# Two transformer blocks on one core: norm updates in two halves of the tokens, and a second output unit issued ahead

## Chip, cores and metric

The kernel runs on one core of one Trainium2 chip. The metric is device time in microseconds (us); the median of three runs before the change is 2707.68 us (2707.38 to 2710.1).

## The reference, cut to what matters

512 tokens of width 1024 go through two layers of a first block and then through a second block. Everything is fp32. In the first block the result of each matrix is normed before it is added to the residual, and the sum is normed again for the next matrix; these two norms with the addition between them are the "sandwich":

```python
def rms_norm(x, g):
    y = x * lax.rsqrt(jnp.mean(x * x, axis=-1, keepdims=True) + EPS)
    return y * g

for l in range(2):                                   # first block
    h = rms_norm(x, attn_pre_g[l])
    proj = h @ w_in[l]                               # q, k, v of 8 head pairs, and the forget logits
    ...                                              # 4 differential and 4 forgetting head pairs -> mixed
    x = x + rms_norm(mixed @ w_out[l], attn_post_g[l])
    h = rms_norm(x, ffn_pre_g[l])
    y = (silu(h @ w_gate[l]) * (h @ w_up[l])) @ w_down[l]
    x = x + rms_norm(y, ffn_post_g[l])
# second block: x += mixer(rmsnorm(x)); x += (relu(rmsnorm(x) @ w1) ** 2) @ w2, twice
# (first mixer: stick-breaking attention, "SB"; second: gated recurrence, "HG")
```

## The kernel before, in words

**Layout.** Activations lie transposed: the width of 1024 is 8 tiles (KD) of 128 partitions, with the 512 tokens (S) along the free dimension, so each tile is 128x512. A "unit" is one 128-column slice of a weight matrix. It needs 8 k-tiles, and each k-tile takes three fp32r matmuls of 128x512 (high part of the weight with high part of the input, high with low, low with high), 24 in all, into one PSUM bank (`products`, L625).

**Weights.** SP loads a unit's raw weights into one of two slots (`load`, L451), and may do so once the slot's low part before was made. GpSimd rounds them to `w_hi` (`round_unit`, L570, instruction L576), when the unit that used `w_hi` in that slot is done. VectorE makes `w_lo = w_raw - w_hi` (`split_low`, L1167) at a place in its hand-written order, and TensorE waits for that. At a stage's start two more units are kept in `ex_hi`/`ex_lo` (`round_extra`, `split_extra`, L1162) so that four units can be computed side by side.

**Queues.** Each engine runs a program in a fixed order; semaphores join them. So an instruction that waits holds everything behind it on its engine.

**The sandwich.** In the output stage and in the last part of the FFN's down stage VectorE takes each unit out of PSUM into `yT` (`take_y`, L1361), ScalarE squares it, VectorE adds the square to `square_sum` (L1139). After the eighth, TensorE sums over partitions with a matrix of ones (`sum_squares`, L694; an fp32 matmul, issued as two instructions), ScalarE makes `rstd` with Ln and Exp (L1740), and VectorE runs `update_x` (L1344): for each tile j scale `yT` (L1351), low part of the tile before (L1148), every second time the pair of squares (L1156), and add to `xT` (L1359). ScalarE makes `h_hi` and the square of each new tile (L1747). TensorE consumes the tiles in `side_by_side` (L675): units 0 and 1 in the banks acc0 and acc1 at once, units 2 and 3 (the extra ones) in `po` and `sc` or `tp`, three and four tiles behind (LAGS), and between them the four pair sums of the next norm (L646).

**Behind the sandwich.** After the attention's sandwich comes the gate stage: `gate_up` on VectorE (L1382) takes gate and up of one FFN tile, through a chain with four activations on ScalarE; TensorE's unit pair n+1 needs the weights that VectorE splits inside the `gate_up` of the pair before (L1387, L1397). After the FFN's sandwich comes the next layer's attention (or SB): TensorE issues the forget logits' products and the rotation of q and k (L832), VectorE takes q and k (`take_qk`, L1260).

**Stage ends.** `early_output` (L668) makes the first two output units of a mixer, a and b, before the last head pair's output is there: the first 21 matmuls of a and 9 of b are spread over the last pair's work, and the rest follows as `a[21:] + b[9:]`. a[21:] waits for the last head pair (`low_output` L1278, `sb_low` L1489, `hg_low` L1701).

Of the kernel before, what the change touches and what calls it, by code (L numbers as in the profile page):

```python
# [68 lines left out]
def aux_uses():  # L69

    uses = []
    for p in range(-1, PAIRS):
        for k in range(SLOTS):
            if p == -1 and k == 3:
                uses.append("norm_att")
# [8 lines left out]
    uses += ["norm_att_post", "norm_ffn", "norm_ffn_post"]  # L84
# [18 lines left out]
A_M1 = A_SB + 3 * PAIRS + 1  # L103
# [4 lines left out]
LAGS = [0, 0, 3, 4]  # L108
# [17 lines left out]
def added_base(n):  # L126

    return 2 + KD * n

def block2_norm(i):

    return KD * (2 * LAYERS + i), KD * (4 * LAYERS + i), added_base(2 * LAYERS + i - 1)
# [35 lines left out]
def two_blocks(nc, x, positions, attn_pre_g, w_in, forget_bias, lam_q1, lam_k1, lam_q2, lam_k2, diff_sub_g,  # L169
# [3 lines left out]
    with ExitStack() as ctx:  # L173
# [71 lines left out]
        pair_sum = [square_sum, part(5632, 512)]  # L245
        gate = part(5632, 512)
# [64 lines left out]
        unit_done = sem("unit_done")  # L311

# [130 lines left out]
        N_CONSTS = 5 + 4  # L443

# [79 lines left out]
        def _(pool):  # L524
# [72 lines left out]
            with pool.Fori(0, LAYERS) as l:  # L597
# [12 lines left out]
                round_units(half + 2, U_GU0 // 2 - 1)  # L610
                round_extra(half + U_GU0 // 2 + 1)
                for slot in range(2):
                    round_unit(half + U_GU0 // 2 + 2, slot, w_hi[:, slot], 2 * half + U_GU0 + slot + 3)
                round_units(half + U_GU0 // 2 + 3, (U_LAYER - U_GU0) // 2 - 2)
                round_extra(half + U_LAYER // 2 + 1)
# [5 lines left out]
        def _(pe):  # L621
# [3 lines left out]
            def products(bank, hi, lo, w_hi_, w_lo_, k_tiles, done, before=None, after=None):  # L625

                ops = []
                for k in range(k_tiles):
                    for i, (w, r) in enumerate(((w_hi_, hi), (w_hi_, lo), (w_lo_, hi))):
                        def issue(k=k, i=i, w=w, r=r):  # L630
                            if i == 0 and before is not None:
                                before(k)
                            mm = pe.matmul(bank[:], w[:, k], r[:, k], start=(k == 0 and i == 0),  # L633
                                           stop=(k == k_tiles - 1 and i == 2))
                            if k == k_tiles - 1 and i == 2:
                                mm.then_inc(done, 1)
                            if i == 2 and after is not None:
                                after(k)
# [3 lines left out]
            def sum_pair(n, q):  # L642

                pe.wait_ge(pair_added, n + q + 1)
                last = q == KD // 2 - 1
                pe.matmul(aux[:], ones[:, 0:P], pair_sum[q % 2], start=(q == 0),  # L646
                          stop=last).then_inc(aux_done if last else square_summed, 1)

# [11 lines left out]
            def extra_unit(half, slot, bank, base):  # L660

                def before(k):
                    if k == 0:
                        pe.wait_ge(w_split, 2 * half + slot + 3)
                    pe.wait_ge(h_ready, base + k + 1)
                return products(bank, h_hi, h_lo, ex_hi[:, slot], ex_lo[:, slot], KD, unit_done, before)

            def early_output(half, ready, base):  # L668
# [4 lines left out]
                return a[:n] + b[:EARLY], a[n:] + b[EARLY:]  # L673

            def side_by_side(half, base, n, banks):  # L675

                units = [unit(half, i, h_hi, h_lo, ready=h_ready, base=base, fresh=True) for i in range(2)]
                units += [extra_unit(half + 1, i, bank, base) for i, bank in enumerate(banks)]
                for k in range(KD + LAGS[len(units) - 1]):
                    if k in (2, 4, 6, KD - 1):  # L680
                        sum_pair(n * (KD // 2), (k - 1) // 2 if k < KD - 1 else KD // 2 - 1)
                    for ops, lag in zip(units, LAGS):
                        if 0 <= k - lag < KD:
                            run(ops[3 * (k - lag):3 * (k - lag) + 3])
# [425 lines left out]
        def _(v):  # L1110
# [40 lines left out]
            def add_pair(n, norm, j):  # L1151

                v.wait_ge(square_ready, n + j + 1)
                if j > 3:
                    v.wait_ge(square_summed, 3 * norm + j // 2 - 1)
# [18 lines left out]
            for j in range(KD):  # L1174
# [4 lines left out]
                if j % 2:  # L1179
                    add_pair(0, 0, j)  # L1180
# [949 lines left out]
```

## Time and profile before

| | before |
|---|---|
| median of three runs | 2707.68 us |
| the profiled execution | 2704.35 us |
| its span in the profile | 2702.6 us |
| mean granted TensorE clock | 0.985 |
| TensorE matmul busy | 2606.3 us (96%) |
| TensorE weight loads busy | 2058.9 us (76%) |
| VectorE busy | 1651.4 us (61%) |
| ScalarE busy | 748.6 us (28%) |
| GpSimd busy | 456.5 us (17%) |
| TensorE in the chain that ended last | 84% |

### The profile page before, as it was taken

To read this page: it belongs to the slowest core of one execution; us is meant where nothing else is said; L and a number is where in the kernel's file an instruction comes from. 1 tells how busy PE (TensorE), PEld (TensorE's weight loads), DVE (VectorE), ACT (ScalarE), POOL (GpSimd) and SP (SyncE) were. 2 spreads that over 40 slices of the span, in tenths; PEclk is the share of its full clock that TensorE was granted. 3 is DMA by queue.
4 is the path that set the end of the run, shared out by engine and by line. 5 is a ranking of instruction groups with operands and counts; after the bars stand their busy time and mean duration, and the time that the engine had idled before them with its cause. 6 is when DMAs were issued, how large, how long until landed. Compare 5 with 4: busy or idle time off the path is not lost.

```text
span 2702.6 us, 38398 instructions
## 1 busy us (share of the span) xinstructions
PE 2606.3 (96%) x12250; PEld 2058.9 (76%) x12250; DVE 1651.4 (61%) x2625; ACT 748.6 (28%) x1391; POOL 456.5 (17%) x454
## 2 busy tenths in 40 slices
PE   8999899999899989999899989999999999999999
PEld 5776688887577668888766658888888887788887
DVE  6754666454775566645567776544458888564452
ACT  3333232120333333212145541100025555210000
POOL 4111111112111111212201101111211111112111
PEclk9999999999899999999989999999999999999999
DMA  3221233333122123333312113333332221233333
GB/s 110 55 63 53 76 90 100 94 97 99 48 62 63 55 70 98 96 94 101 93 40 63 54 32 93 101 94 95 99 94 63 63 62 47 78 94 101 93 101 94
DMA packets 417270, 214.80 MB, mean 79 GB/s; under 512 B 6819, under 2 KB 416014, under 8 KB 417166
## 3 DMA queue, kind: packets, MB, share of 16 engines
q1 hardware_dynamic: 416144, 212.89, 27.3%
q8 instruction: 59, 0.97, 0.2%
q10 hardware_dynamic: 1022, 0.58, 0.1%
q14 instruction: 45, 0.37, 0.0%
HBM read 211.34 MB, written 2.10 MB: 79 GB/s over the span
## 4 chain that ended last, share of the span: by engine, by line
PE 84%; DVE 7%; ACT 4%; issue 3%; POOL 1%; DVEq 0%; ACTq 0%; POOLq 0%
PE acc L633 71%; PE sc L740 2%; PE sc L1051 1%; PE tp L633 1%; PE tp L763 1%; PE po L786 1%; PE po L633 1%; ACT scratch L1916 1%; ACT scratch L1914 1%; DVE scratch L1440 1%; PE aux L646 1%; PE tp L902 1%; DVE xT L1359 1%; DVE w_lo L1170 1%; PE po L773 0%
## 5 line engine op out<-in xcount | busy, mean ns | idle before, releaser
L633 PE MATMUL acc<-h_hi,w_hi 128*128 128x512 f32 x1968 | 811.0, 412 | 31.0 <-DVE h_lo L1148 24.4
L576 POOL TENSOR_SCALAR w_hi<-w_raw 128x1024 fp32r<-128x1024 f32 x390 | 418.7, 1074 | 2200.4 <-PE acc L633 2130.3
L633 PE MATMUL acc<-h_lo,w_hi 128*128 128x512 f32 x1968 | 775.0, 394 | 0.0
L633 PE MATMUL acc<-h_hi,w_lo 128*128 128x512 f32 x1968 | 775.0, 394 | 0.0
L1170 DVE TENSOR_TENSOR w_lo<-w_raw,w_hi 128x1024 fp32r<-128x1024 f32 x390 | 477.6, 1225 | 76.3 <-POOL w_hi L576 76.2
L633 PEld LDWEIGHTS acc<-h_hi,w_hi 128*128 128x128 f32 x1968 | 373.2, 190 | 142.6 <-issue 40.4
L633 PE MATMUL acc<-mid_hi,w_hi 128*128 128x512 f32 x1120 | 440.4, 393 | 7.3 <-DVE mid_lo L1701 3.2
L633 PE MATMUL acc<-mid_lo,w_hi 128*128 128x512 f32 x1120 | 440.0, 393 | 0.0
L633 PE MATMUL acc<-mid_hi,w_lo 128*128 128x512 f32 x1120 | 438.2, 391 | 0.0
L633 PEld LDWEIGHTS acc<-h_lo,w_hi 128*128 128x128 f32 x1968 | 373.8, 190 | 80.5 <-issue 10.6
L633 PEld LDWEIGHTS acc<-h_hi,w_lo 128*128 128x128 f32 x1968 | 372.8, 189 | 81.6 <-issue 1.4
L633 PEld LDWEIGHTS acc<-mid_hi,w_hi 128*128 128x128 f32 x1120 | 211.0, 188 | 55.6 <-DVE w_lo L1170 4.6
L633 PEld LDWEIGHTS acc<-mid_lo,w_hi 128*128 128x128 f32 x1120 | 211.4, 189 | 45.2 <-issue 2.4
L633 PEld LDWEIGHTS acc<-mid_hi,w_lo 128*128 128x128 f32 x1120 | 211.2, 189 | 44.3 <-issue 0.8
L1513 DVE TENSOR_TENSOR xT<-xT,acc 128x512 f32 (+1 forms) x80 | 55.0, 688 | 201.7 <-PE acc L633 201.7
L1977 ACT ACTIVATE mid_hi<-scratch 128x512 f32 x64 | 40.5, 633 | 471.9 <-DVE scratch L1552 471.9
L1549 DVE TENSOR_TENSOR scratch<-acc,rstd 128x512 f32<-128x512 f32 x64 | 44.3, 692 | 130.5 <-PE acc L633 122.0
L1295 DVE CUSTOM_DVE_ANT_0 scratch<-sc,mask_row 128x128 f32<-128x128 f32 (+3 forms) x128 | 62.4, 487 | 80.8 <-PE sc L740 41.3
L1827 ACT ACTIVATE scratch<-scratch,stat 128x128 f32<-128x128 f32 (+3 forms) x128 | 72.0, 563 | 134.7 <-DVE stat L1295 134.7
L1885 ACT ACTIVATE mid_hi<-scratch 128x512 f32 x44 | 27.8, 632 | 202.9 <-DVE scratch L1400 202.9
L1738 ACT ACTIVATE scratch<-yT 128x512 f32 x32 | 20.2, 632 | 208.7 <-DVE yT L1368 137.4
L1393 DVE TENSOR_TENSOR scratch<-acc,rstd 128x512 f32<-128x512 f32 x42 | 29.0, 691 | 76.4 <-PE acc L633 76.4
(316 smaller groups left out, 2665.1 us busy)
## 6 DMA issues: line engine op xcount, KB each, us to landing
w_raw<-in_mlp_w_dram SPq DMA_DIRECT2D x128, 512.0 KB, 4.1
w_raw<-in_w_in_dram SPq DMA_DIRECT2D x48, 512.0 KB, 3.9
w_raw<-in_w_gate_dram SPq DMA_DIRECT2D x44, 512.0 KB, 3.7
w_raw<-in_w_up_dram SPq DMA_DIRECT2D x44, 512.0 KB, 3.7
w_raw<-in_w_down_dram SPq DMA_DIRECT2D x32, 512.0 KB, 4.1
w_raw<-in_hg_w_in_dram SPq DMA_DIRECT2D x32, 512.0 KB, 4.0
w_raw<-in_sb_w_qkv_dram SPq DMA_DIRECT2D x24, 512.0 KB, 3.8
w_raw<-in_w_out_dram SPq DMA_DIRECT2D x16, 512.0 KB, 4.1
```

The source lines that it names most:

```text
L576: nc.gpsimd.tensor_scalar(to, w_raw[:, slot], 1.0, 1.0, ALU.mult, ALU.mult).then_inc(w_rounded, 1)
L633: mm = pe.matmul(bank[:], w[:, k], r[:, k], start=(k == 0 and i == 0), stop=(k == k_tiles - 1 and i == 2))
L646: pe.matmul(aux[:], ones[:, 0:P], pair_sum[q % 2], start=(q == 0), stop=last).then_inc(aux_done if last else square_summed, 1)
L740: mm = pe.matmul(sc[m][:, 0:n], qT[p % 2][r, t * P:t * P + P], kT[p % 2][r, 0:n], start=True, stop=(p < NDIFF))
L1170: TT(w_lo[:, slot], w_raw[:, slot], w_hi[:, slot].bitcast(F32), ALU.subtract).then_inc(w_split, 1)
L1295: v.tensor_tensor_reduce(prob[k % 4][:, 0:n], sc[k % 2][:, 0:n], mask_row[:, S - n:S], 1.0, BIG, ALU.add, ALU.min, stat[:, k % 4:k % 4 + 1 ...
L1393: TT(up, banks[1][:], rstd[:], ALU.mult).then_inc(evacuated[1], 1)
L1513: TT(dst, dst, acc[slot][:], ALU.add).then_inc(evacuated[slot], 1)
L1549: TT(gate, acc[i][:], rstd[:], ALU.mult).then_inc(evacuated[i], 1)
L1827: ACTV(prob[k % 4][:, 0:n], prob[k % 4][:, 0:n], ACT.Exp, bias=stat[:, k % 4:k % 4 + 1], scale=-1.0, accum_out=stat[:, 4 + k % 4:5 + k % 4 ...
L1885: ACTV(mid_hi[:, c % 2, ds(j, 1)], hid, ACT.Copy).then_inc(mid_hi_ready, 1)
L1977: ACTV(mid_hi[:, c % 2, ds(2 * m + i, 1)], hid, ACT.Copy).then_inc(mid_hi_ready, 1)
```

## The change

- Both norms of each sandwich, and the first norm of the kernel, work on two halves of 256 tokens. The last two units of the output and down stages are computed in the order unit 0 first half, unit 1 first half, unit 0 second half, unit 1 second half (`last_pair`), and VectorE takes each half by itself. The sum over partitions is made once for each half (`sum_half`).
- `update_x` becomes `normed_update`: a loop over both halves, with the low part two tiles behind instead of one.
- `side_by_side` runs each unit in two halves, 256 columns per matmul. In the first half units 0 and 1 lead and 2 and 3 follow by two and three tiles; in the second half 2 and 3 lead and 0 and 1 follow.
- Units 0 and 1 of a stage now have the extra weight buffers, units 2 and 3 have `w_hi`/`w_lo`, so that the fifth unit's weights can be rounded when unit 2 is done. The splits move in VectorE's order accordingly. Units 0 and 1 go to `sc` and `sc`/`tp` instead of the acc banks.
- `early_output` issues 12 more matmuls of b ahead of a's last three.

```diff
-LAGS = [0, 0, 3, 4]
+FIRST_LAGS = [0, 0, 2, 3]
+SECOND_LAGS = [2, 3, 0, 0]
+HALF = S // 2
@@ GpSimd, start
-            for slot in range(2):
-                round_unit(0, slot, w_hi[:, slot], None)
-            round_extra(1)
+            round_extra(0)
+            for slot in range(2):
+                round_unit(1, slot, w_hi[:, slot], None)
@@ TensorE
+            def last_pair(half, hi, lo, k_tiles, added, a_n, taken):
+                def of(i, h):
+                    def before(k):
+                        if k == 0 and h == 0:
+                            pe.wait_ge(w_split, 2 * half + i + 3)
+                            pe.wait_ge(evacuated[i], half)
+                        if k == 0 and h == 1:
+                            pe.wait_ge(half_taken, taken + i + 1)
...
+                run(of(0, 0))
+                run(of(1, 0))
+                ops = of(0, 1)
+                run(ops[:14])
+                pe.wait_ge(aux_free, a_n)
+                sum_half(added + KD, 0)
+                run(ops[14:])
+                run(of(1, 1))
+                pe.wait_ge(aux_free, a_n + 1)
@@ early_output
-                return a[:n] + b[:EARLY], a[n:] + b[EARLY:]
+                return a[:n] + b[:EARLY], b[EARLY:n] + a[n:] + b[n:]
@@ side_by_side
+                for h, lags in ((0, FIRST_LAGS), (1, SECOND_LAGS)):
+                    units = [of(n, h) for n in range(count)]
+                    for k in range(KD + max(lags[:count])):
+                        if h == 0 and k == 3:
+                            sum_half(added, 1)
+                        for q, at in enumerate((5, 6, 7, 9) if h == 0 else (3, 4, 6, 7)):
+                            if k == at:
...
+                                sum_pair(norm, h, q)
+                        for n in ((0, 1, 2, 3) if h == 0 else (2, 3, 0, 1)):
+                            if n < count and 0 <= k - lags[n] < KD:
+                                run(units[n][3 * (k - lags[n]):3 * (k - lags[n]) + 3])
@@ VectorE, start
+            for h in range(2):
+                for j in range(KD):
+                    low_half(0, h, j, gains[:, G_ATT_PRE + j:G_ATT_PRE + j + 1])
+                    if h == 0 and j == 0:
+                        split_extra(0, 0)
+                        split_extra(0, 1)
...
+                    if h == 0 and j in (2, 4):
+                        split_low(1, j // 2 - 1)
@@ VectorE, sandwich
+                def normed_update(g, n, half, following, first):
+                    take_half(half, 0, 0, n, first)
+                    split_extra(following, 0)
+                    add_half(n, 0, 0, 0)
+                    take_half(half, 1, 0, n, first)
+                    add_half(n, 0, 1, 1)
+                    split_extra(following, 1)
+                    take_half(half, 0, 1, n, first)
+                    add_half(n, 1, 0, 2)
...
+                    for h in range(2):
+                        c = columns(h)
+                        v.wait_ge(rstd_ready, l * 8 + 2 * g + 3 + h)
+                        for j in range(KD + 2):
+                            if j < KD:
+                                STT(yT[:, j, c], yT[:, j, c], layer_gain[:, g, j:j + 1], rstd[:, c], ALU.mult,
+                                    ALU.mult).then_inc(y_scaled, 1)
+                            if j >= 2:
+                                low_half(norm, h, j - 2, layer_gain[:, g + 1, j - 2:j - 1])
...
+                            if h == 0 and j == 2:
+                                take_half(half, 1, 1, n, first)
+                                split_low(following + 1, 0)
+                            if h == 0 and j == 3:
+                                add_half(n, 1, 1, 3)
+                            if h == 0 and j == 4:
+                                split_low(following + 1, 1)
@@ gate stage, VectorE
-                            gate_up(0, acc, 2)
+                            gate_up(0, (sc[0], tp[0]), 2, 2)
@@ ScalarE: in both_norms and at the start, second half
+                        if j == 2:
+                            inv_rms(a_n + 2, D, columns(0))
```

`take(half, slot, behind)` waits for `behind` more units to be done; in the gate stage `gate_up(0)` therefore waits for the third finished unit, which is unit 0.

## Rows read from the trace of the kernel before

**Rows 1.** Waits of TensorE, whole span; total us, times, longest.

```profile
PE acc L633 <- DVE h_lo L1148: 24.4, 12, 4.6
PE aux L698 <- DVE scratch L1143: 10.1, 4, 2.6
...
PE acc L633 <- DVE mid_lo L1701: 3.2, 1, 3.2
PE acc L633 <- DVE mid_lo L1492: 2.2, 1, 2.2
```

**Rows 2.** Timeline (start, length), TensorE, first attention sandwich: last output matmul to last side-by-side.

```profile
296.73 0.39 PE L633 MATMUL acc<-mid_hi,w_lo 128*128 128x512 f32 x1
299.61 1.13 PE L698 MATMUL aux<-scratch,ones 128*128 128x512 f32 x2 [2.50 <-DVE scratch L1143]
305.23 0.80 PE L633 MATMUL acc<-h_hi,w_hi 128*128 128x512 f32 x1 [4.49 <-DVE h_lo L1148]
...
335.23 0.39 PE L633 MATMUL sc<-h_hi,mid_lo 128*128 128x512 f32 x1
```

**Rows 3.** Busy time and clock in a window: PE, PEld, DVE, ACT, POOL, PEclk, DMA.

```profile
302.00:308.00 6.00, 2.77 (x6) 1.82 (x6) 5.68 (x7) 2.61 (x5) 1.33 (x1) 0.50 0.29 86
```

**Rows 4.** Timeline, TensorE: eight fp32 matmuls of 128 columns and what follows them.

```profile
2028.91 1.13 PE L1035 MATMUL sc<-yT 128*128 128x128 f32 x8
2029.88 0.60 PE L1040 MATMUL aux<-ident,yT 128*128 128x128 f32 x4
```

**Rows 5.** Groups by line and form: half-width operations of VectorE and ScalarE (busy, mean ns).

```profile
L1598 DVE TENSOR_TENSOR cosT<-yT 128x256 f32<-128x256 f32 x24 | 10.0, 416 | 0.0
L1916 ACT ACTIVATE scratch<-scratch 128x256 f32<-128x256 f32 x8 | 3.4, 419 | 0.3
```

**Rows 6.** Timeline, VectorE and GpSimd, first attention sandwich: last split, one collision.

```profile
288.60 1.22 DVE L1170 TENSOR_TENSOR w_lo<-w_raw,w_hi 128x1024 fp32r<-128x1024 f32 x1
...
304.74 1.33 POOL L576 TENSOR_SCALAR mid_hi<-w_raw 128x1024 fp32r<-128x1024 f32 x1 [3.15 <-DMA w_raw<-in_w_up_dram]
...
305.09 1.52 DVE L1359 TENSOR_TENSOR xT<-xT,yT 128x512 f32<-128x512 f32 x1
```

**Rows 7.** Timeline, VectorE and TensorE: start of the first three `gate_up`, unit pair waiting.

```profile
329.63 0.69 DVE L1386 TENSOR_TENSOR scratch<-acc,rstd 128x512 f32<-128x512 f32 x1 [4.34 <-PE acc L633]
...
345.64 1.22 DVE L1170 TENSOR_TENSOR w_lo<-w_raw,w_hi 128x1024 fp32r<-128x1024 f32 x1
...
346.91 0.50 PE L633 MATMUL acc<-h_hi,w_hi 128*128 128x512 f32 x1 [0.42 <-DVE w_lo L1170]
```

**Rows 8.** Timeline, TensorE: first FFN sandwich and the one before SB, first and last marks.

```profile
676.46 1.21 PE L698 MATMUL aux<-scratch,ones 128*128 128x512 f32 x2 [2.57 <-DVE scratch L1143]
...
713.30 0.39 PE L633 MATMUL tp<-h_hi,mid_hi 128*128 128x512 f32 x1
...
1345.19 1.12 PE L698 MATMUL aux<-scratch,ones 128*128 128x512 f32 x2 [2.57 <-DVE scratch L1143]
...
1375.75 0.39 PE L633 MATMUL tp<-h_hi,mid_lo 128*128 128x512 f32 x1
```

**Rows 9.** Timeline, kernel start: TensorE's first unit and the end of side-by-side, GpSimd's extra roundings.

```profile
16.51 0.79 PE L633 MATMUL acc<-h_hi,w_hi 128*128 128x512 f32 x1 [5.75 <-DVE w_lo L1170]
...
20.73 1.61 POOL L576 TENSOR_SCALAR mid_hi<-w_raw 128x1024 fp32r<-128x1024 f32 x1 [5.43 <-DMA w_raw<-in_w_in_dram]
24.41 1.18 POOL L576 TENSOR_SCALAR mid_hi<-w_raw 128x1024 fp32r<-128x1024 f32 x1 [2.06 <-DMA w_raw<-in_w_in_dram]
...
44.35 0.39 PE L633 MATMUL tp<-h_hi,mid_lo 128*128 128x512 f32 x1
```

**Rows 10.** Timeline, end of the first attention: last low part, end of unit a, next unit.

```profile
258.07 0.69 DVE L1281 TENSOR_TENSOR mid_lo<-yT,mid_hi 128x512 fp32r<-128x512 f32 x1 [0.70 <-ACT mid_hi L1813]
...
259.87 0.39 PE L633 MATMUL acc<-mid_hi,w_lo 128*128 128x512 f32 x1
...
264.18 0.50 PE L633 MATMUL acc<-mid_hi,w_hi 128*128 128x512 f32 x1 [0.53 <-DVE w_lo L1170]
```

More of the change, by code:

```diff
@@ L623, in _, with products @@
             pe.sem_inc(wf_done, 1)
-            def products(bank, hi, lo, w_hi_, w_lo_, k_tiles, done, before=None, after=None):
+            def products(bank, hi, lo, w_hi_, w_lo_, k_tiles, done, before=None, cols=slice(0, S)):
                 ops = []
@@ L672, in early_output, with side_by_side, of, before @@
                 n = 3 * (KD - 1)
-                return a[:n] + b[:EARLY], a[n:] + b[EARLY:]
[L675 to L684, printed above, removed]
+                return a[:n] + b[:EARLY], b[EARLY:n] + a[n:] + b[n:]
+            def side_by_side(half, norm, banks, added, a_n):
+                def of(n, h):
+                    def before(k):
+                        if k == 0 and h == 0:
+                            pe.wait_ge(w_split, 2 * half + n + 3)
+                        pe.wait_ge(h_ready, 2 * KD * norm + KD * h + k + 1)
+                    high, low = ((ex_hi, ex_lo) if n < 2 else (w_hi, w_lo))
+                    return products(banks[n], h_hi, h_lo, high[:, n % 2], low[:, n % 2], KD,
+                                    unit_done if h else None, before, columns(h))
+                count = len(banks)
+                for h, lags in ((0, FIRST_LAGS), (1, SECOND_LAGS)):
[5 more added lines that the diff above has]
+                            if k == at:
+                                if q == 0:
+                                    pe.wait_ge(aux_free, a_n + h)
+                                sum_pair(norm, h, q)
+                        for n in ((0, 1, 2, 3) if h == 0 else (2, 3, 0, 1)):
+                            if n < count and 0 <= k - lags[n] < KD:
+                                run(units[n][3 * (k - lags[n]):3 * (k - lags[n]) + 3])
             def share(work, k, n):
@@ L1342, in _, with take_half @@
                 low_output(PAIRS - 1)
[L1344 to L1359 removed]
+                def take_half(half, slot, h, n, first):
+                    if h == 0:
+                        v.wait_ge(half_done, 2 * n + slot + 1)
+                    else:
+                        take(half, slot)
+                    dst = yT[:, KD - 2 + slot, columns(h)]
+                    done = evacuated[slot] if h else half_taken
+                    if first:
+                        COPY(dst, acc[slot][:, columns(h)]).then_inc(done, 1)
+                    else:
+                        TT(dst, dst, acc[slot][:, columns(h)], ALU.add).then_inc(done, 1)
@@ L1381, in _, with gate_up @@
                     if kind == "gu":
-                        def gate_up(j, banks, splits):
+                        def gate_up(j, banks, splits, behind=0):
                             g = l * FF1_TILES + first + j
-                            v.wait_ge(rstd_ready, l * 4 + 3)
-                            take(half + j, 0)
+                            v.wait_ge(rstd_ready, l * 8 + 6)
+                            take(half + j, 0, behind)
                             TT(gate, banks[0][:], rstd[:], ALU.mult).then_inc(evacuated[0], 1)
@@ L1448, in take_raw @@
                         v.wait_ge(sb_qk_ready, 2 * p + 2 + i)
-                    take(half + u // 2, u % 2)
-                    bank = po if u == 3 and not previous else acc[u % 2]
+                    take(half + u // 2, u % 2, 1 if par < 0 else 0)
+                    bank = sc[i] if par < 0 else po if u == 3 and not previous else acc[u % 2]
                     TT(raw, bank[:], rstd[:], ALU.mult).then_inc(evacuated[u % 2], 1)
@@ L1779, in first_gain @@
                 return gains[:, G_ATT_PRE + j:G_ATT_PRE + j + 1]
-            pre_norm(0, 0, first_gain)
-            inv_rms(0, D)
+            a.sem_inc(aux_free, 1)
+            for j in range(KD):
+                pre_tile(0, 0, j, first_gain(j))
+            for j in range(KD):
+                if j == 2:
+                    inv_rms(1, D, columns(0))
+                pre_tile(0, 1, j, gains[:, G_ATT_PRE + j:G_ATT_PRE + j + 1])
+            inv_rms(2, D, columns(1))
             a.wait_ge(vec_consts, 4)
```

227 lines of the change are left out of this document (128 added, 99 removed).

## The prediction

> **What bounds the kernel now.** I read the page's busy table, TensorE's waits, then the timelines of the places where it waits. TensorE is 96% busy, and its chain ends last, so time can only be won where it stands still, runs at half clock, or waits for the first tile of a stage. Of its waits [rows 1], two groups belong to the norms: 24.4 us for `h_lo` and 10.1 us for `square_sum`. At the first attention sandwich the last output matmul starts at 296.73, the sum at 299.61, the first product at 305.23, the last side-by-side one at 335.23 [rows 2]. From 296.96 to 335.46 there are 38.5 us for 96 matmuls at 0.2275 (the distance of starts) and five sums at 0.86, 26.1 us: 12.4 us are lost. VectorE is busy all of 302 to 308, and the clock granted there is 0.50, 1.2 GHz [rows 3]. The FFN's sandwich (673.89 to 713.30) and the one before SB (1342.62 to 1375.98) lose about as much [rows 8]. This is what the change is after; four sandwiches lose some 48 us.
>
> **Price of a half.** A VectorE or ScalarE operation of 256 elements takes 0.42 us where 512 take 0.69 and 0.63 [rows 5]; in sequence I count 0.335 for a half addition and 0.39 for a half scalar_tensor_tensor. A tile of the update (scale, low, add, half a pair sum) then costs VectorE 1.29 us per half. No fp32r matmul of 256 columns is in the trace. The nearest rows are eight fp32 ones of 128 columns, each of which passes its columns twice: 0.97 us, 0.121 each [rows 4]. Bounds are 0.107 (256 columns at 2.4 GHz) and 0.135 (that and twice the 14 ns by which 0.2275 is over 512 columns). I take 0.120, near the row, so two halves cost 0.0125 more than one whole; a half sum costs 0.43.
>
> **A page's rule on this.** The Trainium skill, page "TensorE: Matmul & The Clock Gate", section "Back-to-back issue gap", gives a columns/2.4 + 2.5 ns gap, 109 ns for 256 columns. By its form 512 columns would take 216 ns; this trace shows 227.5.
>
> **Attention sandwiches (two).** Times as in the first. (a) `last_pair` starts where the two units start now, 286.04. Unit 0's first half takes 24 x 0.12 = 2.9, to 288.95. Unit 1 then needs its low part, whose split starts at 288.60 and ends at 289.82 [rows 6]: TensorE waits 0.9, as half the work covers the split no longer. Unit 1's first half ends at 292.8. Take, square and add of it (three steps of 0.42 with 0.1 between) are done at 294.5, when 14 matmuls of the next half are too, so the sum hides. Unit 0 ends at 296.2, unit 1 at 299.1. (b) VectorE in order: add, second extra split (its weights land 4.1 after the slot is free, at 293.95), take and add of the next half; the first scaling is at 297.9, now 302.16. The low part two behind gives `h_lo` at 300.35. TensorE waits 1.25. (c) Between low parts 0 and 1 now stand the take of the last half and a split of 1.2, then an addition that waits for a square, then another split: low parts 1, 2, 3 end at 302.95, 305.35, 307.6. TensorE has only 0.72 (two units) and 1.09 (three) per tile there, and waits 1.9, 1.65, 0.75. (d) From then on it is bound by itself: 10.8 for the rest of the first half and 13.3 for the second (96 x 0.12, four sums). Side-by-side ends at 331.7, 3.8 earlier.
>
> (e) What is queued behind. Now unit 0 ends long before the others, so `gate_up(0)` starts at 329.63, right after `rstd`, and the splits for the sixth pair end at 346.86, when TensorE has waited 0.42 [rows 7]: 17.2 from the start of the chain of three `gate_up`. After the change units 2 and 3 end first and unit 0 just before the last, so the chain starts at 331.7, with TensorE's work over. TensorE waits 1.8 for the fifth unit's split (it stands behind the first addition), computes two units, and waits again until 331.7 + 17.2 = 348.9, now 346.9. So the 3.8 us are paid back: +2.0 us. I price one collision per sandwich of GpSimd's rounding with a VectorE addition, as an addition takes 1.52 instead of 0.69 beside a rounding [rows 6]: +0.4 beyond those now. Sum +2.4 each, +4.8.
>
> **The rule of the port.** The Trainium skill, page "SBUF — State Buffer", section "Who interferes with whom", says that a VectorE instruction with two SBUF inputs and a GpSimd one that reads SBUF block each other whole. The 1.52 agrees. Additions of halves are shorter than a rounding, and by that rule each collision could cost up to a whole rounding.
>
> **FFN sandwich before attention (one).** Same steps with 18 matmuls per unit: start 665.7, 1.4 us wait for the split, first extra weights land only at 669.5, first scaling 676.95, plus 33.8 as above: 710.75 against 713.30 [rows 8]. Behind it the rotation waits for unit 0, done only now: +0.4. Sum -2.2, with a collision -1.8.
>
> **Sandwich before SB (one).** Three units, VectorE bound: first scaling 1345.7, plus 28.7 = 1374.4, now 1375.98 [rows 8]: -1.6, with a collision -1.2. Behind it the q and k norm chain is unchanged.
>
> **Start.** Side-by-side now runs from 16.51 without a wait to 44.58. Units 2 and 3 have weights that land late: GpSimd rounds them at 20.73 and 24.41 [rows 9]. Now they are asked for after 24 and 36 whole matmuls. After the change unit 2 is asked for after 18 half ones, at 20.4 even at half clock, and its split ends at 23.6: 3.2 us wait. Unit 3's ends at 26.9: 1.3 more. The rest of the first half takes 9.6, to 36.5, the second 13.3: 49.8, +5.2. ScalarE's `inv_rms` at j = 2 waits for the first half's last sum, so low parts end at about 41.4 instead of 29.9, and the setup of constants behind them (9.4 us on VectorE) becomes late: forget weights split at 50.4, rotation at 52.3, now 46.1. I take +6.2.
>
> **Stage ends.** In attention a's last three matmuls (from 259.41) have no wait: the last low part ends at 258.76 [rows 10]. Twelve b matmuls ahead put them 2.73 later. The next unit in a's slot starts 4.1 after a's last matmul (take, square, addition, split: 260.09 to 264.18), and b's remaining three cover 0.7 of that where 15 covered 3.4. So the next unit is 2.73 later: two times, +5.5. Before the HG output the wait is 3.18 [rows 1], filled by the twelve, but the same 4 us chain behind a shows in its place: 0. Before the SB output the wait is 2.18: +0.5.
>
> **Sum.** 4.8 - 1.8 - 1.2 + 6.2 + 5.5 + 0.5 = +14.0 us. On the profiled execution: 2704.35 + 14.0 = 2718.4. That execution lies 3.3 below the median of the runs, so on the median: 2707.7 + 14.0 = 2721.7, rounded to 2721.
>
> **Rivals.** (1) Not slower: halves run at the array's pace. Place: all stretches bound by TensorE, some 160 half matmuls per sandwich of four units and as many at the start. At 0.109 each of four such places gains 1.8 us, the last pairs and SB 2 more, 9 in all: 2712, within 0.2% of before. It decides from about 0.111 down. The page's gap above is this rival. For it: the weight load beside a matmul is short enough at 0.121 in [rows 4]; against: that 0.121 itself, and the 14 ns that whole matmuls show over their columns. (2) Faster: the queue behind the gate stage is loose. If the third `gate_up` is taken 5 us sooner relative to the first (or TensorE's pair n+1 does not hang on it), each attention sandwich keeps 3.8 instead of paying 2: -11.6. With half of rival 1: 2702 or less. For it: TensorE waits only 0.42 there now; against: 0.42 means just that the chain has no slack. (3) Slower still: half clock. Waits of 2 to 4 us now stand behind side-by-side and at the stage ends, and half clock followed waits of this length now [rows 3]; six places at 1 to 3 us each: 2728 to 2738. (4) It does not do what it says: b ahead covers nothing, since the split chain is behind a. That is in the forecast; were it wrong, 5.5 us go: 2715.
>
> **Chances.** Forecast with (4), 2712 to 2728: 0.50. (1): 0.15, within 0.2% (5.4 us, about what a measurement of this kernel can tell from no change). (2): 0.14. (3): 0.16. Others to both sides 0.05. So faster by over 0.2% (below 2702.3) 0.17, within 0.18, slower 0.65. The range leaves out the outer parts of (2) and (3): 2700 to 2732.
>
> **What would show it.** Right: the sum's wait gone; `h_lo` waits split into several of 1 to 2 us; TensorE waiting for `w_lo` right behind the first attention side-by-side (about 2 us) and 11 us later (about 4); for `w_lo` at 20 and at 25 us; 3.4 us for `w_lo` after the first output pair. Half matmuls 0.12 apart. Wrong: a distance of 0.11 or less, `gate_up(0)` starting well before side-by-side ends, or no wait between the first and second output pair.

## The result, and the profile after

The changed kernel takes 2750.57 us (median of 4 runs, 2743.93 to 2751.58), the kernel before 2708.36 beside it (2707.38 to 2710.1): ratio 1.0153, 95% interval 1.0139 to 1.0166. It is slower, as forecast, but by 42 us where 14 were forecast, and outside the range. The profiled execution took 2750.34, its span is 2748.6 us at a mean granted clock of 0.977, against 2702.6 at 0.985.

Waits of TensorE in the changed kernel, whole span (total us, times, longest), as [rows 1]:

```profile
PE acc L654 <- DVE w_lo L1237: 28.5, 12, 3.9
PE sc L654 <- DVE h_lo L1214: 22.9, 12, 4.6
...
PE aux L671 <- DVE scratch L1433: 1.7, 3, 0.7
```

The kernel before, same view:

```profile
PE acc L633 <- DVE w_lo L1170: 8.5, 6, 5.8
```

The wait for the sum of squares (10.1 us) is down to 1.7, as the change means to. The waits for `h_lo` stay (24.4, now 22.9). For low parts of weights TensorE waited 8.5 us before, 5.8 of them at its first unit; now it waits 28.5, and none of them is that first one (5.5 us, listed under another tile). So some 26 us of such waits have come.

Timeline of TensorE (start, length, instruction), changed kernel: end of the first attention stage, as [rows 10], and the first halves of the last pair, as [rows 2].

```profile
272.63 0.39 PE L654 MATMUL acc<-mid_hi,w_lo 128*128 128x512 f32 x1
276.31 0.79 PE L654 MATMUL acc<-mid_hi,w_hi 128*128 128x512 f32 x1 [3.29 <-DVE w_lo L1237]
276.90 0.63 PE L654 MATMUL acc<-mid_lo,w_hi 128*128 128x512 f32 x1
277.33 0.63 PE L654 MATMUL acc<-mid_hi,w_lo 128*128 128x512 f32 x1
...
282.44 0.40 PE L654 MATMUL acc<-mid_hi,w_lo 128*128 128x512 f32 x1
282.68 0.40 PE L654 MATMUL acc<-mid_hi,w_hi 128*128 128x512 f32 x1
...
301.05 0.28 PE L654 MATMUL acc<-mid_hi,w_hi 128*128 128x256 f32 x1
301.16 0.28 PE L654 MATMUL acc<-mid_lo,w_hi 128*128 128x256 f32 x1
301.28 0.28 PE L654 MATMUL acc<-mid_hi,w_lo 128*128 128x256 f32 x1
301.40 0.28 PE L654 MATMUL acc<-mid_hi,w_hi 128*128 128x256 f32 x1
```

The wait of 3.29 us is the one forecast (3.4). Behind it the matmuls start 0.43 apart until 282.44, then 0.23: until then they run at 1.2 GHz, the lower of TensorE's two clock levels, called half clock below. The same work of TensorE in the two kernels (window, its length, busy, matmuls, clock, DMA share, GB/s); first the kernel before, from 264.2 (next unit) to 286 (last pair), then the changed one, from 276.3 to 301:

```profile
264.20:286.00 21.80, 21.80 (x96) 1.00 0.33 96
```

```profile
276.30:301.00 24.70, 24.69 (x96) 0.88 0.29 85
...
366.00:376.00 10.00, 10.00 (x34) 0.74 0.36 105
```

The same 96 matmuls take 2.9 us more. The second window of the changed kernel lies behind the longest new wait of the gate stage, 3.57 us at 365.80.

Because most work is the same in both kernels, the same instruction can be found in both traces. How much later it comes in the changed one, and by how much that grows in each stage, gives the ledger. It compares one profiled execution of each kernel; that of the kernel before is 4 us below its median (us; the markers are in the time of the kernel before; "filled ends" and "all filled" are experiments below):

```
stage (markers)                      forecast  changed  filled ends  all filled
start (0 to 65)                         6.2       9.6        9.5        10.4
1st attention end to gate (240-500)     5.1      11.7        7.7         5.1
FFN sandwich (661-800)                 -1.8       2.4        1.9         0.6
2nd attention end to gate (900-1100)    5.1      11.6        8.7         6.9
before SB (1300-1404)                  -1.2       2.4        2.0         2.2
SB end (1580-1700)                      0.5       3.3       -0.5        -0.5
HG end (2200-2400)                      0         5.0        1.7         3.1
all, whole span                        14        46.0       30.0        27.0
```

The forecast for an attention stage is 2.7 for its end and 2.4 for its sandwich. No stage is better than forecast, and the two attention stages, where the forecast put both kinds of new wait, miss by 13 of the 32 us.

### The profile page after: what moved, and what is told of

Read it like the earlier page. It is cut to its first block, busy times and chain, and to the rows that moved or that the text cites. A ratio compares the mean times of both kernels' runs of the same rounds, so it can differ in the third digit from the quotient of the medians.

```text
span 2748.6 us, 40155 instructions
## 1 busy us (share of the span) xinstructions
PE 2636.0 (96%) x12924; PEld 2122.5 (77%) x12924; DVE 1667.2 (61%) x2766; ACT 767.3 (28%) x1497; POOL 453.0 (16%) x454
## 4 chain that ended last, share of the span: by engine, by line
PE 82%; DVE 8%; issue 4%; ACT 4%; POOL 1%; DMA 1%; DVEq 0%; ACTq 0%; POOLq 0%; SPq 0%
PE acc L654 68%; PE sc L1111 2%; PE sc L795 2%; PE sc L654 2%; PE tp L654 1%; DVE w_lo L1237 1%; PE po L654 1%; PE tp L818 1%; PE po L841 1%; ACT scratch L2049 1%; ACT scratch L2047 1%; PE tp L962 1%; PE aux L665 1%; DVE scratch L1548 1%; DVE scratch L1366 0%
## 5 line engine op out<-in xcount | busy, mean ns | idle before, releaser
L654 PE MATMUL acc<-h_hi,w_hi 128*128 128x512 f32 x1888 | 767.0, 406 | 9.7 <-DVE w_lo L1237 9.7
L654 PE MATMUL acc<-h_hi,w_lo 128*128 128x512 f32 x1888 | 740.9, 392 | 0.0
L654 PE MATMUL acc<-h_lo,w_hi 128*128 128x512 f32 x1888 | 740.7, 392 | 0.0
L654 PE MATMUL acc<-mid_hi,w_hi 128*128 128x512 f32 (+1 forms) x1176 | 454.4, 386 | 19.3 <-DVE w_lo L1237 18.8
L654 PE MATMUL acc<-mid_lo,w_hi 128*128 128x512 f32 (+1 forms) x1176 | 453.4, 386 | 0.0
L654 PE MATMUL acc<-mid_hi,w_lo 128*128 128x512 f32 (+1 forms) x1176 | 452.7, 385 | 0.0
L654 PEld LDWEIGHTS acc<-h_hi,w_hi 128*128 128x128 f32 x1888 | 356.9, 189 | 105.8 <-issue 29.2
L654 PEld LDWEIGHTS acc<-h_hi,w_lo 128*128 128x128 f32 x1888 | 356.0, 189 | 77.7 <-issue 1.4
L654 PEld LDWEIGHTS acc<-h_lo,w_hi 128*128 128x128 f32 x1888 | 356.9, 189 | 73.5 <-issue 6.2
L2012 ACT ACTIVATE scratch<-scratch 128x512 f32<-128x512 f32 x44 | 27.8, 632 | 173.5 <-DVE scratch L1494 173.5
```

The lines of the kernel that those rows point to most:

```text
L654: mm = pe.matmul(bank[:, cols], w[:, k], r[:, k, cols], start=(k == 0 and i == 0), stop=(k == k_tiles - 1 and i == 2))
L2012: steps(ACTV(gate_t, gate, ACT.Abs))
```

## The experiments

Theory A: half clock behind the new waits, priced too low in the forecast as its third rival, carries the missing time. Theory B: waits cost their own length, and something else is missing.

**Order back.** The changed kernel with the old order of the first output pair:

```diff
-                return a[:n] + b[:EARLY], b[EARLY:n] + a[n:] + b[n:]
+                return a[:n] + b[:EARLY], a[n:] + b[EARLY:]
```

> The changed kernel with the old order of the first output pair at the four stage ends. Theory A (half clock: the 3.3 to 3.9 us waits that the new order brings are followed by stretches at the 1.2 GHz level, and these carry most of the time that the forecast missed): the chain of the order, 6.0 us by the forecast's own term, plus about 3 us of half clock at each of three ends and 1.5 us at the fourth, together 16 to 18 us less than the changed kernel, about 2733 us. Theory B (the waits cost their own length and no more): 6 us less, about 2744 us, and TensorE's granted clock in the 36 us around the last output pair of an attention stage stays near 0.91.

2732.55 us (2731.04 to 2734.97), ratio to before 1.009 (1.0073 to 1.0107): 18.0 us less than the changed kernel, and clear of its range. Its timeline at the same place:

```profile
272.57 0.39 PE L654 MATMUL acc<-mid_hi,w_lo 128*128 128x512 f32 x1
273.46 0.50 PE L654 MATMUL acc<-mid_hi,w_hi 128*128 128x512 f32 x1 [0.51 <-DVE w_lo L1237]
273.80 0.39 PE L654 MATMUL acc<-mid_lo,w_hi 128*128 128x512 f32 x1
```

The wait is 0.51 and the clock stays up. One line of ordering costs three times what its chain of waits does (6 us by the forecast).

**Order only.** The kernel before with this line alone changed, the other way round.

> The kernel before with the new order of the first output pair alone. Theory A: the time rises by 13 to 17 us (6 of chain, the rest half clock behind the waits), to about 2723 us, and the granted clock behind the first output pair of an attention stage falls from 1.00 to about 0.9. Theory B: it rises by 6 us, to about 2714 us.

2722.74 us (2717.41 to 2725.11), ratio 1.0049 (1.0031 to 1.0066): +14.3 us against 6 for the chain. Behind its first output pair:

```profile
267.41 0.50 PE L633 MATMUL acc<-mid_hi,w_hi 128*128 128x512 f32 x1 [3.29 <-DVE w_lo L1170]
268.56 0.63 PE L633 MATMUL acc<-mid_lo,w_hi 128*128 128x512 f32 x1
268.98 0.63 PE L633 MATMUL acc<-mid_hi,w_lo 128*128 128x512 f32 x1
```

Both directions agree with A and not with B.

**Filled ends.** The changed kernel, whose new waits stay, with work in them that nobody needs:

```diff
+            def fill(bank, n):
+                for _ in range(n):
+                    pe.matmul(bank[:], mid_hi[:, 0, 0, 0:P], mid_hi[:, 0, 0], start=True, stop=True)
...
                 run(rest)
+                fill(tp[0], 12)
```

> The changed kernel with 12 idle products of 512 columns (2.7 us at the 0.2275 us of one at full clock) put on TensorE in front of the wait for the weights at the four stage ends; they write a bank that nobody reads, and the wait of 3.3 to 3.9 us is filled. Theory A: the clock stays at its upper level behind the wait, 2.5 to 3 us come back at each of three ends and 1.5 at the fourth, 9 to 10 us in all, about 2741 us. Theory B: nothing comes back, 2750 us, since the products only fill a wait.

2735.44 us (2730.98 to 2740.88), ratio 1.0103 (1.0083 to 1.0123): 15.1 us back, for doing more work. The chain of weights did not move; only the clock did:

```profile
272.80 2.88 PE L710 MATMUL tp<-mid_hi 128*128 128x512 f32 x12
276.27 0.50 PE L654 MATMUL acc<-mid_hi,w_hi 128*128 128x512 f32 x1 [0.59 <-DVE w_lo L1244]
276.61 0.39 PE L654 MATMUL acc<-mid_lo,w_hi 128*128 128x512 f32 x1
276.84 0.40 PE L654 MATMUL acc<-mid_hi,w_lo 128*128 128x512 f32 x1
```

The first real matmul starts at 276.27 where it started at 276.31, and the ones behind it are 0.23 apart. This is the cleanest evidence for A: same release, other clock. By the ledger the stages with the ends give 4.0, 2.9, 3.8 and 3.3 us. Instruction by instruction, 2.8, 2.7, 1.7 and 1.6 us of this, 8.8 in all, stand right behind the four waits, which is what was expected. The rest lies in stretches whose code is the same in both kernels; "What stays uneven" returns to it.

**Filled gate.** The same 12 products ahead of `gate_up(half + 2, 1)`, reading `h_hi`.

> The changed kernel with 12 such idle products in front of the fifth unit of the gate stage, in both layers, where TensorE waits 3.57 us for the low parts of the weights. Theory A: about 2.4 us come back in each layer, 5 us in all, about 2746 us. Theory B: nothing comes back, 2750 us.

2744.98 us (2742.69 to 2745.16), ratio 1.0133 (1.0116 to 1.015): 5.6 us less, which the ranges of the two kernels (the changed one's begins at 2743.93) do not separate. The expectation put them at the wrong wait: ahead of the fifth unit TensorE waits 1.28 us, the 3.57 us are ahead of the seventh. The trace still shows an effect. The products run longer than the 1.28 us, so the fifth and sixth units are later and the wait ahead of the seventh is 2.61 us. Behind it the matmuls start 0.23 apart in both layers, and the 2.5 and 2.4 us that half clock adds there in the changed kernel are 0.2 and 0.2.

**Before, filled.** The kernel before with `fill(tp[0], 9)` ahead of and `fill(tp[0], 16)` behind `sum_squares` in the four layer sandwiches.

> The kernel before with idle products of 512 columns (nobody reads them) around the sum of squares behind each output and down product of the layers: 9 in the wait in front of it (2.0 us of a wait of 2.57) and 16 in the wait behind it (3.6 us of a wait of 4.5). Four places. Theory A (half clock behind a wait costs time): the gate stage's first units run at the upper level, and of the 10 us at granted clock 0.66 and the 13 us at 0.51 that stand there now 1 to 2 us come back per place, the rest being set by VectorE's low parts: 4 to 8 us less than before, about 2702 us. Theory B: those units wait for VectorE tile by tile anyway, so nothing comes back: 2708 us.

2706.75 us (2701.64 to 2711.78) against 2707.52, ratio 0.9996 (0.9986 to 1.0006): nothing. The windows of the first attention and the FFN sandwich of the kernel before, then the same work in this kernel:

```profile
302.00:312.00 10.00, 5.57 (x15) 0.66 0.35 104
...
677.00:690.00 13.00, 7.49 (x17) 0.51 0.32 85
```

```profile
303.00:313.00 10.00, 6.91 (x23) 0.88 0.35 103
...
677.80:690.80 13.00, 8.74 (x33) 1.00 0.32 85
```

The clock rose from 0.66 and 0.51 to 0.88 and 1.00, and the FFN sandwich did not get shorter (the shift of later instructions stays at 0.8 us through it): VectorE's tiles set the pace there. So half clock is not a price by itself. It costs its share where TensorE is the bound behind the wait, and nothing here, where TensorE is fed tile by tile. Here B was right.

**All filled.** The changed kernel with both fills above, 20 fp32 products ahead of the loop over the layers, 8 or 16 products behind `last_pair`, and 12 and 6 of 256 columns at k = 1 and 2 of the first half of `side_by_side`.

> The changed kernel with idle products in all its long TensorE waits: the 12 at each of the four stage ends and the 12 ahead of the fifth gate unit of the two kernels above, 20 products of 128 fp32 columns in the 5.5 us wait at the start, 8 or 16 behind the last output or down pair, and 12 and 6 of 256 columns between the first tiles of the side-by-side units. Theory A: the half clock goes almost wholly; the stage ends give 15 us and the gate 5.6 us as measured, the start 3 us, the two norms of each layer 1 to 2 us each: about 2723 us, granted clock 0.99. What is then left over the kernel before, 14 us, should be the forecast's chain. Theory C (the idle products themselves cost as much where VectorE feeds TensorE tile by tile): no better than the sum of the two kernels above, 2729 us.

2730.6 us (2727.5 to 2733.78), ratio 1.009 (1.0073 to 1.0107), clock 0.992: 20.0 us back, no more than the two fills alone gave (20.7). Theory C was nearer than A for the extra ones, in line with the run before. In the ledger's last column the first attention stage now grows by 5.1 us, what the forecast's chain gave: 2.8 at its end and 2.4 in its sandwich. The second grows by 6.9, and 1.8 of that is half clock behind the 2.61 us ahead of its seventh unit.

**Start filled.** Only the 20 products at the start:

```diff
+            for _ in range(20):
+                pe.matmul(acc[0][:, 0:P], ident[:], ident[:], start=True, stop=True)
             with pe.Fori(0, LAYERS) as l:
```

> The changed kernel with 20 products of 128 fp32 columns in the 5.5 us wait at the start alone. Theory A: 3 us come back (the start lost 9.6 us where 6.2 were forecast), 2747.5 us. Rival: the start's excess is in the chain of GpSimd's and VectorE's weights and nothing comes back, 2750.5 us.

2743.59 us (2738.98 to 2748.18), ratio 1.0144 (1.0127 to 1.0161). The median fell by 7, but not at the start: the score that began at 74.80 in the changed kernel begins at 74.68.

```profile
74.68 1.13 PE L803 MATMUL sc<-scratch 64*128 64x512 f32 x4 [2.47 <-DVE stat L1374]
```

The fill did raise the clock, but moved the half clock to another place. Windows of TensorE, changed kernel, then this one:

```profile
22.00:28.00 6.00, 4.74 (x23) 0.63 0.43 117
52.00:60.00 8.00, 7.47 (x21) 0.79 0.24 66
```

```profile
22.00:28.00 6.00, 4.61 (x18) 0.52 0.41 113
52.00:60.00 8.00, 6.20 (x22) 1.00 0.25 66
```

From 16 to 22 the clock is 1.00 instead of 0.50, but TensorE then waits 3.63 us for unit 2's low part instead of 1.85, and runs slower behind it; the last low part and the setup behind it come 1.2 us later. Behind the 2.54 us wait for the forget weights the clock stays up, where the changed kernel has half clock behind its 2.55, and that gives the 1.2 us back. So half clock has a price at the start too, and this run shifts it but does not remove it. The 11 us that this profiled execution (2738.98) is shorter lie behind the start, most at the gates and ends, where the code is the same.

**Old order, filled.** Old order with all fills but those at the ends.

> The changed kernel with the old order of the first output pair and with all idle products except those at the stage ends. Theory A: 2732.5 us less 5.6 for the gate, 3 for the start and 1 to 2 us for each of the four norms: about 2718 us. Theory C: 2727 us.

2723.89 us (2720.31 to 2725.96), ratio 1.0061 (1.0045 to 1.0078): 8.7 less than order back, between the two theories.

**No turns.** The changed kernel without the six operations between `ang` and `red`, which take whole turns off the angles (a part of the computation left out):

```diff
-            steps(TS(turn, ang, 1 / (2 * math.pi), None, ALU.mult))
...
-            steps(STT(red, turn, -c3, red, ALU.mult, ALU.add))
-            steps.wait()
-            TS(red, red, -pi_in, pi_in, ALU.max, ALU.min).then_inc(vec_consts, 1)
+            TS(red, ang, -pi_in, pi_in, ALU.max, ALU.min).then_inc(vec_consts, 1)
```

> The changed kernel without the six VectorE operations that take whole turns off the angles (3.6 us at the start; the angles are left as they are, so sine and cosine are of other values). Theory S (at the start the path goes through VectorE's setup of constants, which now stands behind the last low part at 42.1 us, and through the forget weights' split behind it, 51.25 us): the split ends 3.6 us sooner, TensorE's wait of 2.55 us for it goes, and the score that started 9.6 us later than before starts about 6.5 us later: 2747 us. Rival (half clock at the start, or the sum of squares of the second half at 46.8 us, sets it): the start stays 9.6 us late, 2750 us.

2745.31 us (2743.05 to 2747.96), ratio 1.0137 (1.012 to 1.0154), a range that overlaps the changed kernel's. In the profiled execution the start is 2.2 us shorter, where 3.1 were expected. Timeline of VectorE, changed kernel, then this one:

```profile
41.70 0.43 DVE L1222 TENSOR_TENSOR scratch<-scratch 128x256 f32<-128x256 f32 x1
...
51.25 1.23 DVE L1355 TENSOR_TENSOR mid_hi<-wf_raw,mid_hi 128x1024 fp32r<-128x1024 f32 x1
52.40 0.68 DVE L1336 SCALAR_TENSOR_TENSOR yT<-sc,rstd 128x512 f32<-128x512 f32 x1
53.00 1.22 DVE L1237 TENSOR_TENSOR w_lo<-w_raw,w_hi 128x1024 fp32r<-128x1024 f32 x1
54.69 0.69 DVE L1343 TENSOR_TENSOR yT<-aux,sinT 128x512 f32<-128x512 f32 x1 [0.48 <-PE aux L887]
```

```profile
47.80 0.51 DVE L1279 TENSOR_TENSOR lconst<-scratch 128x1 f32<-128x1 f32 x1 [3.07 <-ACT scratch L1883]
...
50.44 1.22 DVE L1343 TENSOR_TENSOR mid_hi<-wf_raw,mid_hi 128x1024 fp32r<-128x1024 f32 x1
```

With VectorE's work gone, the forget weights' split moved by 0.8 us only, since VectorE then waits 3.07 us for ScalarE's exponential, which stands behind the root of the second half. The other 1.4 us are not the edit's: behind the forget weights this execution ran at a clock of 1.00 (52 to 60) where the changed kernel has 0.79. The kernel of the next experiment, whose start is that of the changed one, also ran at 1.00 there, after the same wait of 2.55 us, and its start is 1.5 us shorter (8.1). So two chains lie within a microsecond of each other at the start: VectorE's setup, and ScalarE behind the last sum of squares (46.8 us, in the kernel before 37.25).

**Filled at the seventh unit.** 14 products between `gate_up(half + 2, 1)` and the loop behind it, in front of the wait of 3.57.

> The changed kernel with 14 idle products of 512 columns (3.2 us) in front of the seventh gate unit of each layer, where the 3.57 us wait is (the 12 of the earlier kernel stand in front of the fifth unit, where the wait is 1.28 us). Theory A: the units behind the wait start with 0.23 us between matmuls instead of 0.43, 2 to 3 us come back per layer, 5 us in all: 2745.5 us. Theory B: nothing: 2750.5 us.

2743.04 us (2738.78 to 2746.86), ratio 1.013 (1.0114 to 1.0147): 7.5 less, again not clear of the changed kernel's range. The ledger is: right behind the seventh unit's wait the changed kernel loses 2.5 and 2.4 us, this one 0.0 and 0.0, and the matmuls start 0.23 apart. That is 4.9 us for the fill, within the 4 to 6 expected. The two attention stages together grow by 6.1 us less (8.2 and 9.0 instead of 11.7 and 11.6); the 1.2 us over the 4.9, and what the median has beyond that, lie where the code is the same.

**Old order, filled at the seventh.**

> The same 14 idle products with the old order of the first output pair. Theory A: 2732.5 us less 5: about 2727.5 us, and from the last output pair to the steady gate units the stage is longer than before by what the forecast gave the sandwich, 2.4 us, not by the 5 us of the kernel with the old order alone. Theory B: 2732.5 us.

2726.83 us (2725.16 to 2731.33), ratio 1.0069 (1.0053 to 1.0086): 5.7 less than order back, with ranges that just touch. From 240 to 500 its profiled execution grows by 2.8 us over the kernel before, from 900 to 1100 by 4.1, where order back has 4.8 and 4.9 and the forecast's sandwich 2.4.

**What stays uneven.** Half clock does not cost the same each time. Windows of TensorE behind the first attention end's wait of 3.29 us, changed kernel, then the kernel with only its start filled, whose code and wait there are the same:

```profile
276.30:283.10 6.80, 6.79 (x17) 0.55 0.53 154
```

```profile
276.30:283.10 6.80, 6.80 (x30) 1.00 0.52 154
```

The first loses 2.8 us behind this wait, the second nothing. In the six profiled executions with this order and no fill at the ends, the two attention ends lost 0 to 2.8 us each, 2.0 on average, behind the same 3.3 us. Behind the 3.57 us ahead of the seventh gate unit, where nothing was filled, five executions lost 1.6 to 2.5 us each time, 2.0 on average.

The HG stage shows it in a stretch that the change leaves alone. Windows of TensorE ahead of the HG output, kernel before, then the changed one, 41 us later:

```profile
2279.00:2299.00 20.00, 16.45 (x89) 0.83 0.03 9
```

```profile
2320.00:2340.00 20.00, 18.26 (x71) 0.50 0.03 8
```

The changed kernel falls 3.2 us further behind here. Order back falls 2.5 behind here, order only 3.7, and the others between 1.4 and 4.3, in code that is the kernel before's; the kernel before with its waits filled does not. What makes the half clock start earlier here was not isolated. So a single term of the ledger is uncertain by about 3 us. The median of four executions can move by more: that of the start-filled kernel is 7 us below the changed one's though its start gained nothing. The 14 to 18 us of the order line and the 15 us of the filled ends are clear of this; the 5 to 8 us of the gate fills rest on the traces, not on the medians.

## Why the prediction was right or wrong

The waits of TensorE in the changed kernel that the forecast named, in its timeline:

```profile
23.05 0.58 PE L654 MATMUL po<-h_hi,w_hi 128*128 128x256 f32 x1 [1.85 <-DVE w_lo L1237]
...
317.00 0.39 PE L654 MATMUL sc<-h_hi,mid_hi 128*128 128x256 f32 x1 [1.98 <-DVE h_lo L1214]
...
319.59 0.39 PE L654 MATMUL sc<-h_hi,mid_hi 128*128 128x256 f32 x1 [1.61 <-DVE h_lo L1214]
...
351.08 0.49 PE L654 MATMUL acc<-h_hi,w_hi 128*128 128x512 f32 x1 [1.28 <-DVE w_lo L1237]
...
365.80 0.80 PE L654 MATMUL acc<-h_hi,w_hi 128*128 128x512 f32 x1 [3.57 <-DVE w_lo L1237]
...
2356.66 0.50 PE L654 MATMUL acc<-mid_hi,w_hi 128*128 128x512 f32 x1 [3.88 <-DVE w_lo L1237]
...
2358.08 0.63 PE L654 MATMUL acc<-mid_hi,w_lo 128*128 128x512 f32 x1
```

**Right.** Half matmuls start 0.12 apart (301.05 to 301.40): the first rival, 0.109, falls. Nearly all of the sum's wait went. Most waits came where they were forecast: 3.29 us behind the first output pair (3.4 forecast), 1.28 for the fifth gate unit (1.8), 3.57 for the seventh (4). The first four waits for `h_lo` were forecast as 1.25, 1.9, 1.65 and 0.75 us and came as 1.98, 1.61, 1.07 and none. The low parts are 2.6, 2.4 and 2.3 us apart, as forecast, but the first is 1.6 us late, and TensorE, at half clock from 320, needs longer per tile and so waits less. At the start unit 2 waited 1.85 us (3.2 forecast) and unit 3 0.21 (1.3). That b's matmuls ahead cover nothing at the attention ends is right too: the chain there made the next unit 2.8 us later (2.73 forecast).

The second rival, a loose queue behind the gate, falls as well, since the waits for the fifth and seventh units pay back what side-by-side gains. But this gain was small. From the last pair's start to the end of side-by-side the forecast has 3.8 us less than before; the changed kernel takes 48.75 us (301.05 to 349.80), 0.7 less, and the all-filled one 47.1, 2.3 less. That the sandwich of the all-filled kernel grows by the 2.4 us of the forecast is partly luck: side-by-side ends 1.4 us later than forecast, and the chain behind it takes 16.4 us instead of 17.2. The price of collisions, 0.4, was a little low: two half operations of the first attention sandwich took 1.20 and 1.26 us, 0.8 over their length, where the kernel before has one addition of 1.52.

**Wrong: half clock as a rival and not as a term.** This is the step that failed. The sum priced each new wait at its own length and treated [rows 3] as something that could happen. The changed kernel lost, beyond the chains, 8.8 us behind the waits of the four stage ends, 4.9 behind the gate's second wait in the two layers, 2.9 in the two attention sandwiches (against the all-filled kernel) and 1.5 at the start: 18 us, and 20.0 came back where everything was filled. The third rival had six places at 1 to 3 us each and a chance of 0.16. Its size per place was right, 2.8 us behind the first attention end and 2.0 on average; but it was set against the forecast, where it had to be added, and it had six places where there are nine. Forecast and measured half clock make 2708.4 + 14 + 20 = 2742 us. Even the rival's own range, 2728 to 2738, ends 12 us below the result.

The HG end shows the same slip in small: the forecast set it at 0, as the new wait takes the place of an old one. Of that chain it was right: in the changed kernel the second output pair is only 0.2 us further behind than the work ahead of it. But the new wait, 3.88 us at 2356.66, is followed by matmuls 0.43 apart from 2358.08 on, which cost 1.6 us, and 3.2 us came ahead of the output, as shown above.

The Trainium skill, page "TensorE: Matmul & The Clock Gate", section "HAM oscillation — how this bites in real kernels", tells of a kernel whose bursts each start at the lower clock behind a wait for data, and takes half of the throttled time as the extra wall time. By this, (1 - clock) times the span would be the loss: 63 us here, 22 in the all-filled kernel, so 41 to win. 20.0 were won. In the kernel before the same sum promises 22 us (0.985 to 0.993) and 0.8 were won. The rule holds where TensorE is the bound, as at the attention end (0.12 of 24.70 us is 3.0, and 2.9 were lost); over the whole of this kernel it is too high, and the measurements decide.

**Wrong: the start, 6.2 forecast, 9.6 measured.** The low parts end at 41.7 as forecast (41.4). But the step "the setup of constants behind them becomes late ... rotation at 52.3" left out what stands between. The setup ends 0.8 later. The 1.9 us that it has from the forget weights' split to the rotation hold the split and the q evacuation, but not the split of the next weights (1.22 us, at 53.00), so the rotation comes at 54.69. And TensorE waits 2.55 us for the forget weights, which the forecast doesn't have. Half clock behind this wait makes up 1.5 of the 9.6 us; with the same code and the clock at 1.00 the start grew by 8.1, which leaves 1.9 for the missing steps.

**Wrong: the FFN sandwich and the one before SB, -3.0 forecast together, +4.8 measured.** GpSimd and VectorE, changed kernel, FFN sandwich:

```profile
696.06 1.05 POOL L591 TENSOR_SCALAR mid_hi<-w_raw 128x1024 fp32r<-128x1024 f32 x1 [3.97 <-DMA w_raw<-in_w_in_dram]
```

```profile
697.14 1.23 DVE L1232 TENSOR_TENSOR mid_lo<-w_raw,mid_hi 128x1024 fp32r<-128x1024 f32 x1 [2.12 <-POOL mid_hi L591]
...
699.61 1.26 DVE L1452 SCALAR_TENSOR_TENSOR yT<-yT,layer_gain,rstd 128x256 f32<-128x256 f32 x1
```

The second extra weights land late and their split stands ahead of the last take, so the first scaling comes 12.8 us after the last pair's start (686.83), not 11.25. That is 1.5 us. Half clock in the stretch behind (0.57 from 704 to 714) is a part of the rest, since the all-filled kernel grows by 0.6 instead of 2.4; the last 1 us there was not isolated. Collisions cost a little more than forecast: three half operations of 1.25 to 1.26 us, 0.8 over their length, where the kernel before has two additions of 1.52, 0.83 over theirs. That is 0.7 us, not 0.4. In the sandwich before SB no half operation collided, but a split did (2.02 us at 1384.91, where the others take 1.22), and the first scaling is 0.6 us late; some 2 us of its 3.6 were not isolated.

**The sum, and what stays open.** In this pair of profiled executions the 46 us are the forecast's 14, 18 of half clock behind new waits, 3 of half clock ahead of the HG output, 2 of missing steps at the start, 4 in the FFN's sandwich (about 2 of them half clock), 4 before SB, and 1 ahead of the SB output. Open are about 1 us in the FFN's sandwich, 2 before SB and the 1 ahead of the SB output, each of the size by which half clock moves from run to run; and why the half clock ahead of the HG output starts earlier than in the kernel before.

## What to carry to other kernels

Where TensorE is the bound, price a new wait of 3 us at its length and 2 us more, between 0 and 3, for the half clock behind it, as a term of the sum; where another engine feeds TensorE tile by tile, at its length only. Do not read a gain of 5 us in this kernel from four executions: find the place in the trace. Before a reordering that makes both slots of a double buffer come free at once, look at what refills them: here one line that put b's matmuls ahead of a's last three cost 14 to 18 us, and 6 of them were the chain. If such a wait can't be removed, idle products in it can win back the clock, but no kernel of this study with them was measurably faster than the one before.

## What the hardware showed that was not expected

Twelve matmuls whose result nobody reads, four times, made the kernel 15.1 us faster, 8.8 of them right behind the waits that they filled. Raising the mean granted clock of the kernel before from 0.985 to 0.993 made it no faster (0.9996, 0.9986 to 1.0006). And the same code behind the same wait of 3.29 us ran at 2.4 GHz in one execution and for 6 us at 1.2 GHz in another, and waits of 2.55 us were enough for half clock in some executions and not in others.
